# Expert routing in a two-block model step: slots by expert and rank, gather by pairs of pairs, 16 ring slots

## The reference

```python
# second block, end; t is (256, 1024), 4 groups of 8 experts, TOP_K = 2, D_EXPERT = 256
g_sel = jnp.argmax(t @ w_rg + b_rg, axis=-1)                    # one group for each token
e_in = take((t @ w_re + b_re).reshape(-1, 4, 8), g_sel)         # its eight experts
top_v, top_i = lax.top_k(e_in, 2)
w_top = softmax(top_v) * softmax(g_logits)[g_sel]
combine = sum(one_hot(g_sel * 8 + top_i, 32) * w_top)           # (256, 32)
act = silu(t @ w_gate[e]) * (t @ w_up[e]) * combine[:, e]       # for each expert e
h = h + sum over e of act @ w_down[e]
return rms_norm(h, norm_final)
```

## Time and profile before

| | |
|---|---|
| median of 3 runs | 1186.93 us (1184.87 to 1190.35) |
| the profiled execution | 1192.24 us, of which the span of its instructions is 1190.4 |
| mean granted TensorE clock | 0.932 of 2.4 GHz |
| busy, share of the span | PE 86%, PEld 70%, DVE 50%, POOL 52%, ACT 36% |
| moved by DMA | 224.9 MB, mean 189 GB/s |

### The profile page before, as it was taken

How to read it: one execution, slowest core, us unless ns; L and a number is a source line. 1 busy time by engine, 2 the same in 40 slices (tenths; PEclk the granted TensorE clock), 3 DMA queues, 4 the chain that set the end, 5 groups by cost and what they waited for, 6 DMA issues and landing times.

```text
span 1190.4 us, 19506 instructions
## 1 busy us (share of the span) xinstructions
PE 1019.7 (86%) x7452; PEld 836.6 (70%) x7452; DVE 593.8 (50%) x1343; ACT 426.9 (36%) x637; POOL 614.3 (52%) x549
## 2 busy tenths in 40 slices
PE   5898799988967879999999899899985789787773
PEld 4787788887947769999977799798964534333331
DVE  7303237268545765553159885522226646444445
ACT  4543333323225455555444344354432311111111
POOL 5997814456746776663766459888550111111100
PEclk9999898999977889999999999999996989899986
DMA  6554522233333443343443226545425499999990
GB/s 250 173 207 153 201 72 71 89 142 125 133 115 107 146 172 126 126 140 107 142 142 111 100 74 216 192 158 177 167 116 227 198 369 414 421 421 419 419 384 35
DMA packets 31907, 224.90 MB, mean 189 GB/s; under 512 B 3664, under 2 KB 3664, under 8 KB 5072
## 3 DMA queue, kind: packets, MB, share of 16 engines
q1 hardware_dynamic: 30672, 220.07, 49.2%
q10 hardware_dynamic: 1152, 3.67, 0.9%
HBM read 273.01 MB, written 1.05 MB: 230 GB/s over the span
## 4 chain that ended last, share of the span: by engine, by line
POOL 44%; issue 31%; DMA 11%; PE 8%; DVE 4%; ACT 1%; SPq 0%; POOLq 0%; DVEq 0%; ACTq 0%
POOL wlo L524 44%; DMA ring<-in_experts 11%; PE ps L2393 3%; PE ps L2409 2%; DVE yhl L1720 1%; PE ps L2419 1%; PE ps L2345 0%; PE ps L2346 0%; DVE stat L961 0%; PE ps L2378 0%; POOLq L527 0%; ACT yhl L910 0%; DVE stat L964 0%; DVE x L1782 0%; SPq L507 0%
## 5 line engine op out<-in xcount | busy, mean ns | idle before, releaser
L524 POOL TENSOR_TENSOR wlo<-raw,whi 128x512 fp32r<-128x512 f32 x448 | 585.0, 1341 | 300.8 <-ACT whi L580 300.1
L1857 PE MATMUL ps<-xhi,whi 128*128 128x256 f32 x960 | 282.9, 295 | 12.1 <-DVE xlo L1210 4.1
L1858 PE MATMUL ps<-xhi,wlo 128*128 128x256 f32 x960 | 277.0, 289 | 0.0
L1859 PE MATMUL ps<-xlo,whi 128*128 128x256 f32 x960 | 276.6, 288 | 0.0
L580 ACT ACTIVATE whi<-raw 128x2048 fp32r<-128x2048 f32 x112 | 214.0, 1914 | 143.2 <-PE ps L1859 66.1
L1857 PEld LDWEIGHTS ps<-xhi,whi 128*128 128x128 f32 x960 | 190.0, 198 | 16.2 <-issue 7.9
L1858 PEld LDWEIGHTS ps<-xhi,wlo 128*128 128x128 f32 x960 | 189.9, 198 | 1.0 <-issue 0.7
L1859 PEld LDWEIGHTS ps<-xlo,whi 128*128 128x128 f32 x960 | 189.7, 198 | 0.0
L2393 PE MATMUL ps<-ring,xw 128*32 128x256 f32 x1536 | 104.4, 410 | 32.8 <-DMA ring<-in_experts 31.9
L547 POOL COPY xw<-xs 128x256 f32 x48 | 20.7, 458 | 211.5 <-PE ps L2393 164.1
L1807 PE MATMUL ps<-whi,xhi 128*128 128x512 f32 (+3 forms) x298 | 117.2, 393 | 12.6 <-POOL wlo L524 10.7
(11 more groups left out here) (465 smaller groups left out, 1468.8 us busy)
## 6 DMA issues: line engine op xcount, KB each, us to landing
ring<-in_experts SPq DMA_DIRECT2D x144, 1024.0 KB
raw<-in_weights SPq DMA_DIRECT2D x112, 1024.0 KB, 4.9
x<-in_x SPq DMA_DIRECT2D x2, 512.0 KB, 4.5
memt<-in_mem ACTq DMA_DIRECT2D x1, 1024.0 KB, 8.3
out<-xn ACTq DMA_DIRECT2D x4, 256.0 KB, 2.5
decay<-in_decay ACTq DMA_DIRECT2D x1, 512.0 KB, 4.0
npost<-in_norm_post ACTq DMA_DIRECT2D x1, 512.0 KB, 5.3
nfin<-in_norm_final ACTq DMA_DIRECT2D x1, 512.0 KB, 8.2
```

What stands on the lines that cost most here:

```text
L524: ins = pool.tensor_tensor(wlo[:, j, c], raw[:, j, c], whi[:, j, c].bitcast(f32), ALU.subtract)
L1857: mm(o_, wh[:, k, cc], hi[:, k0 + r0 + k, :], start=first, stop=False, skip_group_check=True)
L1858: mm(o_, wl[:, k, cc], hi[:, k0 + r0 + k, :], start=False, stop=False, skip_group_check=True)
L1859: ins = mm(o_, wh[:, k, cc], lo[:, k0 + r0 + k, :], start=False, stop=last, skip_group_check=True)
```

## The change

- **Slots.** A row's place is now 32 x expert + its rank in the expert (a code), and rows of rank 32 and more get codes of "o" tiles (`further`, behind `ws` in pair 0: six operations of 512 elements, then `over_ready`). Neither counts nor offsets are needed for the first pairs. The windows of POOL, `xs`, `wrow`, `wx`, `start`, `mine` and the 512-column masks are gone.
- **Gather.** DVE makes masks for two pairs at a time (`pick_rows`), TensorE gathers 128 columns for them with 16 matmuls to each PSUM bank (`gather`), half in each of the two pairs before, and DVE copies them with the gain to `xw` (`rows_out`).
- **Weights of the slots** come from one small matmul job (`ws`) after pair 0's `act_copy` (`slot_weights`: a dozen small operations and one of 512), and scale y instead of the transposed rows.
- **Pairs in sequence.** One bank for gate and up, one for y, one `yhl`, `ac` and `aT`; `down(j)` stands behind `combine(j - 1)` in the same turn. `y_lo` is two operations on 64 partitions.
- **Ring.** 16 slots in other places; entries 3 to 5 wait for the last raw units, 6 to 11 for `weights_used` = NU - 1, 12 to 15 for NU. A pair's down entries stand right behind its gate and up entries. The "o" pairs stand at other places in the order.
- **End.** The residual is put into PSUM by four fp32 matmuls with the identity in pair 1 (`residual_in`), and the squares and the final product read PSUM.

```diff
-NRING = 13
+NRING = 16
-        if n % 2 == 0 and n or n == 3:
+        if n in (3, 4, 5, 7, 9, 11, 13, 14):
             pairs.append(("o", len(pairs) - n - 1))
 def ring_plan(npair):
+    return [(j, part, u) for j in range(npair) for part in range(3) for u in range(2)]
...
-                if n == 4:
+                if 3 <= n < 6:
+                    sp.wait_ge(lo_ready, NU - 5 + n)
+                if n == 6:
+                    sp.wait_ge(weights_used, NU - 1)
+                if n == 12:
                     sp.wait_ge(weights_used, NU)
...
+            def pick_rows(g, at_, n=2):
+                do(v.tensor_tensor(hit[:, :, 0:n, :], C("iota").unsqueeze(1).unsqueeze(1).to_broadcast([P, 4, n, 2 * TS]),
+                                   at_.rearrange("p n c -> p c n").unsqueeze(3).to_broadcast([P, 4, n, 2 * TS]), ALU.is_equal))
+                sync()
+                v.tensor_tensor(pick[:, g % 2, :, :].rearrange("p t (n s) -> p t n s", n=2), hit[:, 0:2, :, :], hit[:, 2:4, :, :], ALU.add).then_inc(sem("pick_ready"), 1)
+            def rows_out(g, half):
+                dve.wait_ge(sem("gathered"), 2 * g + half + 1)
+                k = slice(4 * half, 4 * half + 4)
+                v.tensor_tensor(xw[:, g % 2, k, :], ps[1 + half][:, :].rearrange("p (k s) -> p k s", k=4),
+                                D("g_moe")[:, k].unsqueeze(2).to_broadcast([P, 4, 4 * TS]), ALU.mult).then_inc(sem("rows_ready"), 1)
...
             def y_lo(j):
+                    ins = v.scalar_tensor_tensor(yhl[other, b, :], ps[3][mine, :], wslot[mine, PLACE[j]:PLACE[j] + 1],
+                                                 yhl[mine, b, :].bitcast(f32), ALU.mult, ALU.subtract)
...
             for j in range(NT):
-                gate(j)
                 if j:
                     y_lo(j - 1)
-                owners(j)
+                gate(j)
+                if j + 2 - j % 2 < NT:
+                    rows_out(j // 2 + 1, j % 2)
                 act_copy(j)
                 if j == 0:
-                    overflow()
+                    slot_weights()
+                    wait_full(dve, ("ws", 0))
+                    release(v.tensor_copy(wslot[:, :], pj(("ws", 0))[:, 0:NPAIR]), ("ws", 0))
+                    wait_done(dve, ("ws", 0))
+                    further()
+                    wait_done(dve, ("pT", 0))
+                owners(j)
+                if j % 2 and j + 3 < NT:
+                    pick_rows(j // 2 + 2, codes[:, j + 3:j + 5, :])
...
+            def gather(g, half):
+                pe.wait_ge(sem("pick_ready"), g + 1)
+                out = ps[1 + half]
+                for k in range(4 * half, 4 * half + 4):
+                    o_ = out[:, 4 * TS * (k % 4):4 * TS * (k % 4) + 4 * TS]
+                    for t in range(TT):
+                        mm(o_, xnh[:, t, k * P:k * P + P], pick[:, g % 2, t, :], start=t == 0, stop=False)
+                        ins = mm(o_, xnl[:, t, k * P:k * P + P], pick[:, g % 2, t, :], start=False, stop=t == 1)
+                ins.then_inc(sem("gathered"), 1)
+            def residual_in():
+                for t in range(TT):
+                    for h in range(2):
+                        mm(ps[4 + 2 * t + h][:, :], ident, x[:, t, 512 * h:512 * h + 512], start=True, stop=False)
...
-            gate_up(0)
-            for j in range(1, NT):
-                gate_up(j)
-                if j >= 2:
-                    combine(j - 2)
-                down(j - 1)
-            act_transposed(NT - 1)
-            combine(NT - 2)
-            down(NT - 1)
+            for j in range(NT):
+                gate_up(j)
+                if j == 0:
+                    code_rows()
+                if j + 2 - j % 2 < NT:
+                    gather(j // 2 + 1, j % 2)
+                act_transposed(j)
+                if j == 0:
+                    weights_of_slots()
+                if j == 1:
+                    residual_in()
+                if j:
+                    combine(j - 1)
+                down(j)
             combine(NT - 1)
```

More of the change, by code:

```diff
@@ L382, in program @@
         xnl = at("xnl", A + 16 * KB, [P, TT, DM], f32r)
[L383 to L392, removed]
@@ L414, in program @@
[L414 to L420, removed]
+        outp = at("outp", A + 8 * KB, [P, TT, DM])
+        a = [A + 24 * KB]
@@ new lines, in small @@
+        def small(name, shape, dt=f32):
+            size = (4 * int(np.prod(shape[1:])) + 31) // 32 * 32
+            if a[0] <= A + 56 * KB < a[0] + size:
+                a[0] = A + 80 * KB
+            t = at(name, a[0], shape, dt)
+            a[0] += size
+            return t
+        rtl = small("rtl", [P, 8, TT * 36])
+        lgt = at("lgt", a[0], [36, S])
+        sg = small("sg", [P, 256])
+        yhl = small("yhl", [P, 2, 512], f32r)
+        oh = small("oh", [P, 2, TT, NEXP])
+        msum = small("msum", [P, TT, NEXP])
@@ new lines, in program @@
+        prod = small("prod", [P, 2, TT, NEXP])
+        cnt = small("cnt", [NEXP, P])
+        flt = small("flt", [NEXP, P])
+        tally = small("tally", [P, 2, NEXP])
+        match = at("match", a[0], [P, NOVER, NEXP])
+        mval = at("mval", a[0] + 2 * KB, [P, NOVER, NEXP])
+        nfin = small("nfin", [P, DM])
+        over = small("over", [P, 2, NOVER])
+        overi = small("overi", [P, 2, NOVER], i32)
+        choice = small("choice", [P, 8, 4])
+        codes = small("codes", [P, NPAIR, 4])
@@ new lines, in program @@
+        upto = small("upto", [P, 4, NPAIR + 1])
+        which_pair = small("which_pair", [P, 4, NPAIR])
+        which_slot = at("which_slot", a[0], [P, 4, P])
+        sT = small("sT", [P, 2, S], f32r)
+        islot = small("islot", [P, P])
+        diag = at("diag", a[0], [P, 4, P])
+        own = small("own", [P, 2 * S])
+        wslot = small("wslot", [P, NPAIR])
+        hit = small("hit", [P, 4, 2, 2 * TS])
+        pick = small("pick", [P, 2, TT, 4 * TS], f32r)
+        posT = small("posT", [P, 2 * S])
@@ new lines, in program @@
+        xw = at("xw", A, [P, 2, 8, 4 * TS])
+        ac = small("ac", [2 * TS, 256])
+        aT = small("aT", [P, 4 * TS])
+        slots = [A + (56 + 8 * i) * KB for i in range(3)]
+        slots += [base + 8 * KB * i for i in (1, 2, 0)]
+        slots += [base + 8 * KB * i for i in (4, 7, 5, 8)] + [base + 80 * KB, base + 96 * KB]
+        slots += [base + 8 * KB * i for i in (3, 6)] + [base + 72 * KB, base + 88 * KB]
+        ring = [at(f"ring{i}", o, [P, UW])[:, :] for i, o in enumerate(slots)]
@@ L923, in _ @@
-            for t in range(TT):
-                for i in range(2):
-                    d = slice(512 * i, 512 * i + 512)
-                    act.wait_ge(sem("out_ready"), 2 * t + i + 1)
-                    act.dma_start(out_d[:, t, d], xn[:, t, d]).then_inc(sem("out_stored"), 16)
+                if j == 0:
+                    copy(("pT", 0), posT[:, :])
+                    wait_done(act, ("ws", 0))
+                y_hi(j)
+            act.wait_ge(sem("combined"), NT)
+            junk = (outp[:, 0, 0:512], outp[:, 0, 512:1024], posT[:, :], own[:, :])
```

391 lines of the change are left out of this document (152 added, 239 removed).

## The result

The changed kernel took 1169.8 us (1165.63 to 1174.19, four runs) against 1188.45 for the kernel before on the same chip: a ratio of 0.9847, 95% interval 0.9802 to 0.9892, so 18.7 us less. Six more runs on another occasion gave 1173.14 us and 0.9872 [0.9832, 0.9912]. The forecast was 1163.5 us, in a range of 1150 to 1192.

The account below looks back on a forecast made before the run. It took expert-weight transfer as the bound, with queue waits delaying it. Head, pairs, ring waits and end summed to a 1167 us span, 1168.8 against the profiled execution; carrying over its 5.3 us above the median gave 1163.5, range 1150 to 1192.

Parts of the forecast that it names:

- The forecast case: Whole kernel: the summed mechanism holds, time between 1158 and 1170 us; chance 0.50.
- pair 0: First expert pair on TensorE, priced at the lower clock up to about 940: 20.7 us.
- 20 pairs without their waits: Later regular pairs, stages in sequence, 8.72 us each: 174.4 us.
- G: Time of a later pair's gather of 16 single-pass, 128-wide matmuls: 1.9 us at 0.12 each, bounds 1.0 to 3.6.
- waits for the ring: TensorE waiting for expert weights at the seventeenth and twentieth pairs, about 2 and 4 us: 6.1 in all.
- y chain: After the last pair: y_hi and hand-overs 1.4, y_lo 1.4, combine 2.05 us.
- close: From the last combine's end to the kernel's end: squares, sums, roots, scaling and landing, 11.2 us instead of 12.5.
- The head: Chain up to the first pair, without counts and with a narrower gather: first pair at 921.7 instead of 933.3.
- A: Rival: each narrow gather matmul costs as much as a wide one, 0.213 to 0.227 us; 1190 to 1195 us; chance 0.22.
- B: Rival: gather nearly free at 0.06 to 0.08 us per matmul, but more transfer waits; 1153 to 1158 us; chance 0.10.
- Transfers: Expert weight stream, 2.51 us per unit through 16 slots: about 20 us idle, last landing 1145 instead of 1157.
- Rival C: Serial pairs dearer by 8% hand-overs per TensorE step, or lower clock in waits; 1172 to 1178 us; chance 0.17.

Follow-up runs that it names:

- gather_twice: Changed kernel with each gather of pairs 2 to 23 computed twice, same result; 1197.59 us, ratio 1.0069.
- ring_late: Changed kernel with ring entries 3 to 15 all issued only after the last router matmul; 1170.55 us, ratio 0.9831.
- before_early: Kernel before with only the early issue of ring entries as weight buffers come free; 1189.59 us, ratio 1.0013.
- before_order: Kernel before with only its overflow pairs moved to later places (4, 5, 7, 8, 10, 11, 13, 14); 1177.72 us, ratio 0.9915.
- order_old: Changed kernel with the overflow pairs at the places of the kernel before; 1172.95 us, ratio 0.9868.
- order_late: Changed kernel with overflow pairs at 4, 5, 7, 8, 10, 11, 13, 14; 1163.5 us, ratio 0.9785.
- gather_one: Changed kernel with 4 of the 16 matmuls kept in each later gather, so those rows are wrong; 1166.0 us, ratio 0.9793.
- ring13: Changed kernel with 13 ring slots in place of 16; 1176.99 us, ratio 0.9868.
- resid_early: Changed kernel with three of the four residual matmuls moved from pair 1 into pair 0; 1167.09 us, ratio 0.9821.
- order_resid: Changed kernel with both later overflow pairs and three residual matmuls moved into pair 0; 1157.47 us, ratio 0.9720.

## Why the prediction was right, and where it was off

The forecast case happened, in its mechanism: a pair costs what was summed, TensorE is the bound at first, and then both run level. None of the rivals did. Step by step, from msum on, in us:

| step | predicted | measured | why |
|---|---|---|---|
| msum to first pair | 10.3 | 12.1 | a gather matmul 0.213 at the lower clock, not 0.18 |
| pair 0 | 20.7 | 18.1 | clock up from about 925; down again behind the wait |
| pair 1 | 12.2 | 12.7 | its first half at the lower clock |
| 20 pairs without their waits | 174.4 | 173.7 | G 1.8, not 1.9 |
| waits for the ring | 6.1 | 8.4 | at the same two pairs |
| last two pairs | 15.8 | 15.5 | |
| y chain | 4.9 | 5.3 | from down's end |
| close | 11.2 | 11.2 | |
| msum to end | 255.6 | 257.05 | |

**The head** was mis-sized by 1.8 us: masks 0.3 later, the 32 gathers and what follows them 7.0 instead of 5.8, the overflow matmuls 0.3 more. The 0.18 came from the transposes of the earlier trace rows, taken as a price at the lower level. They were not at one level: the granted clock is 0.74 around them and 0.52 right behind them (stretches of the kernel before), where 256-wide matmuls came every 0.213 us:

```profile
897.00:899.00 2.00, 1.53 (x8) 1.15 (x8) 0.60 (x2) 1.05 (x3) 0.56 (x1) 0.74 0.00 0
899.80:905.00 5.20, 5.16 (x24) 4.18 (x24) 4.51 (x8) 3.07 (x6) 0.00 (x0) 0.52 0.01 2
```

In the changed kernel the clock is 0.51 from 905 to 925.

**Pair 0** was priced at the lower clock throughout with two terms at full-clock prices (down at 1.7; it took 3.4). In fact the clock rises to full in the first gate_up, the first gather runs at 0.11, and it falls again while TensorE waits 3.25 us for `which_pair`. Pairs 0 and 1 together took 30.9 us against 32.9 predicted, which makes up for the head.

**G**, on which rivals A and B hung, was right: 0.112 us per matmul against 0.12. The choice of the 64-wide stream of the earlier trace rows as nearest neighbour, because both carry a load of 128 columns, is borne out: 64 wide 0.107, 128 wide 0.112, 256 wide 0.12. A nearer row stood in the trace of before and was overlooked, 128-wide fp32 transposes at full clock, (1.91 - 0.27) / 15 = 0.109 apart (one record lasts 0.27):

```profile
556.60 1.91 PE L1903 MATMUL ps<-cst,qm 128*128 128x128 f32 x16
```

The 81 ns of the Trainium skill (TensorE: Matmul & The Clock Gate, Back-to-back issue gap) would, as an estimate, have given G = 1.3 and 22 x 0.5 = 11 us less of TensorE; the trace does not agree, the gather ran at 0.112 us and no row shown here with a load of 128 columns for each matmul is below 0.107. A is refuted by the row, and gather_twice shows what it would have cost: 1197.59 us, just above A's 1190 to 1195.

**Transfers.** The last landing, msum + 233.6 predicted, came at 235.1; the waits stand at the two pairs named and are 3.7 and 4.8 us, not 2 and 4. That it fits so well is in part luck. The prediction had 22 units out at pair 0's end and some 20 us of idle DMA behind it; measured, 20 were out, and of the 20.8 us of idle time about 12.8 lie ahead of 942 and only 8 behind. And "DMA share well under 1 until about 1050" is wrong, all of it lies ahead of 1000. For the kernel before the prediction took the last landing at 1157; the trace has it at 1160.4, so the tail was 30.0 us and not 33.

**What the prediction credited to the wrong part.** It listed the early issue of units 3 to 15 as a part of the gain without pricing it alone. ring_late and before_early show that it gives nothing. And it said of the wait for the overflow work only that SP "needs it only for unit 24"; that the kernel before could have had some 12 us by moving its "o" pairs alone, before_order shows. What is left for slots, gather, single buffers, 16 slots and end over that is 265.4 - 257.05 = 8.4 us of the 22; with one and the same late order it is 265.4 - 253.0 = 12.4, and with one and the same old order 279.0 - 261.9 = 17.1. So the parts don't add up: a late order is worth some 12 us in the kernel before and 5 to 9 once the rest is in place (261.9 against 257.05 and 253.0), and the rest 17 with the old order and 8 to 12 with a late one. The 8.1 us of the tail belong to the rest; slots, gather, buffers and end were not taken apart.

**The number.** The median of 1169.8 lies 6.3 us above the forecast, and that of the second occasion, 1173.14, above the likely band of 1158 to 1170. What failed is the last step, "the difference carried over gives 1163.5": the 5.3 us by which the profiled execution stood above the median of three runs. In later comparisons the median of the kernel before was 1188.59, 1189.08 and 1191.26, only 1.0 to 3.7 us under the profiled execution, so 1.6 to 4.3 of the 5.3 were chance in three runs. The sum without that step, 1168.8 us, is 1.0 us from the median, but that is partly luck: the profiled execution of the changed kernel took 1165.63, the least of the four, as its msum came 4.6 us early, and the steps of the table, off by up to 2.6 us each, cancel to 1.5. One reason for such a spread can be seen: msum comes between 904.9 and 917.2 in the thirteen profiles; order_old has 906.6 and order_late 917.2, and nothing ahead of it differs between them. And behind a wait for the ring the clock falls or stays, which is worth up to 4.8 us.

**Rival C** came true in its mechanism only, and not in its size: the lower clock did come back in the waits of the start (3.25 us, and the 3.4 us of down(0)) in both profiles of the changed kernel, and behind the late waits in all the variants that had such waits (gather_one, ring_late, ring13, order_late, order_old, resid_early) but order_resid, whose longest was 1.4 us, and not in its own.

## What to carry to other kernels

Before a deep rebuild of a stage that is bound by transfers, look at what the queue waits for while it moves nothing: here one line of the order gave back some 12 us, and the early issue into a ring that is full anyway gave nothing. Price an unknown stream of small matmuls by the row that has the same load, and price each step at the clock that it will have; work that fills a wait of TensorE is worth its own time and the slower matmuls behind the wait as well. Make the sum against the profiled execution and count from the point where the change begins; a difference to the median of three runs isn't worth carrying over.

## What was not expected of the hardware

- The width of a matmul hardly counted here up to 256 while each had a load of 128 columns: 0.107 us (64 wide, fp32 records), 0.112 (128 wide, fp32r), 0.12 (256 wide, fp32r) at full clock; at the lower clock the 128-wide one is 0.213, almost twice.
- The length of a wait for the ring didn't tell whether TensorE's granted clock fell. It stayed at 2.4 GHz in both profiles of the changed kernel (3.05 and 3.04 us in each), in ring13 behind 3.03 and in gather_one behind 2.91. It fell to the lower level behind 2.09 and 2.46 us (ring13), 2.58 (order_late), 2.23, 2.95 and 3.04 (order_old), 3.04 and 3.45 (resid_early), 3.04 to 3.05 three times (gather_one), and in ring_late behind one of 3.04 after it had stayed behind one of 3.06. In order_old it rose again before the next down, and two half gate_ups took 3.45 and 3.54 us in place of 1.93: 1.5 us. In ring_late and order_late it rose only in or behind the next down: 4.8 us. Why it falls in one and not in another stays open.
